# Squares of five norms and of the memory's queries and keys: summed by turning and adding along rows instead of by products with a column of ones

## The chip, the cores and the metric

The kernel runs on one core of a Trainium2 chip. The metric is the device time of one execution in microseconds. Before the change it is 3107.8 us, the median of three runs (3105.99 to 3108.2).

## What is computed

One layer of a first block and two layers of a second one, on 512 tokens of width 1024, all in float32. What matters here is the root-mean-square norm, which stands in front of or behind nearly every part:

```
def _rms(x, w):                      # x: tokens x features
    y = x * rsqrt(mean(x * x, axis=-1, keepdims=True) + EPS)
    return y * w

# memory attention, per head h of 4, width 256:
q = _rms((x @ w_in)[:, memory part].reshape(512, 4, 256), mem_q_norm)
k = _rms((_rms(mem) @ mem_w_kv)[:, :1024].reshape(256, 4, 256), mem_k_norm)

# second block, layer l:
h = h + rmsnorm(mix, gains[1])
h = h + rmsnorm(ff,  gains[3])
```

A norm thus needs, for each token, the sum of the squares over 1024 features (over 256 for each head of the memory's queries and keys).

## The kernel before

**Layout.** Activations are held with features on the 128 partitions and tokens along the row: a tile is 128 features x 512 tokens (256 for the memory). The sum over the features is therefore a sum over partitions and over tiles, and the factor of a token is wanted later in every partition.

**Products.** Each float32 product is made of three fp32r ones (high by high, high by low, low by high), recorded on line 752. Weights come in panels of 128x512 over one DMA queue; ScalarE makes the high half (WH, line 2176), GpSimd the low half (WL, line 2573).

**Order.** The program is a list of steps (PLAN, lines 363 to 531), in part written out by hand, which every engine walks through; LATE (532 to 566) moves single steps of VectorE, ScalarE or GpSimd to an earlier or later place in that engine's own order. Each engine's instructions are in order, and waits are semaphores with a mark per event. The eight PSUM banks are handed out by `lend` (line 718): the next tile gets the bank whose last reader comes earliest in the list, and TensorE waits for that reader.

**How a norm is summed.** ScalarE squares a tile. GpSimd adds tile on tile into one (`gather`, 2575). Then TensorE sums over partitions, step "fac":
- For norms whose last square arrives early enough, all tiles are gathered, TensorE turns the four 128x128 quarters (`across`, 816, recorded on line 819), and VectorE adds along the rows of the turned squares, 128x512 to 128x4 (`summed`, 1395, recorded on line 1398). Tokens then lie on partitions.
- For the five norms "nmem", "nab", "ns0", "nco", "ns1" the last square comes late and is not gathered. TensorE multiplies each quarter of the gathered squares by a column of ones (`columns`, 810, recorded on line 752 as PS<-VC,TMP 128x1), then waits for the last square and adds its quarters in the same PSUM columns. The result is one number per token, and VectorE reads it with one small operation (line 1385).
- For the memory's queries ("nqm", four heads) and keys ("nkm"), GpSimd adds the squares of the two tiles of a head in pairs; TensorE makes the columns of head p behind step "mq" or "mkl" 2p+2, the last head's in steps "nqm" and "nkm". One bank stays open for all heads. "nmem" and "nkm" have two quarters, as the memory has 256 tokens.

Behind the sum GpSimd raises it to the power -1/2 (`power`, 2583, line 2573, SM<-SM,VC). Step "bc" on TensorE broadcasts the factor by turning it (`spread`, 829, line 826, PS<-CST,SM), and VectorE's and ScalarE's work on the normed tiles goes on from there.

**The order at the sites of the change.** "ns0" and "ns1": a short product step "pf" 4, "fac", "pf" 5 (six products), "bc", "pf" 6 and 7, then the steps "grow". "nab" is alike, with "pf" 0 to 3. "nco": "fac" right behind the mixer's last product, then "pf" 1, "bc". "nmem": product "mkl" 0, "nqm", "fac", product "mkl" 1, "bc"; on VectorE LATE puts "fac" of "nmem" ahead of "nqm". On GpSimd "nqm" is first.

Of the kernel before, what the change touches and what calls it, by code (L numbers as in the profile page):

```python
# [16 lines left out]
EPS = 1e-6  # L17
# [565 lines left out]
def program(nc, x_in, mem_in, p_in, pos1, pos2, lam_in, vec_in, cst_in, dm_in, wst, out, total, dry=False):  # L583
    blocks = []
    with ExitStack() as ctx:
# [146 lines left out]
        def tensor(e):  # L732
# [77 lines left out]
            def columns(o, col, q, ind, first, nt=4):  # L810

                for t in range(nt):
                    z = mm(o[:, 64 * t + col:64 * t + col + ind.shape[1]], quarter(q, t), ind, first and t == 0, True)
                return z

            def across(o, q):

                for t in range(4):
                    z = e.transpose(quarter(o, t), quarter(q, t), ident)  # L819
                return z  # L820
# [23 lines left out]
            for marks.step, (kind, *i) in enumerate(PLAN):  # L844
                started.append(-(-len(blocks) // PT))
                if kind == "fac":
                    n = i[0]
                    K = NORM[n][2]
                    o = bank("var", n)
                    e.wait_ge(*at("gathered_fin" if n in ("nfin", "n1") else "gathered", n, last(n)))  # L850
                    if last(n) == K - 1:
                        across(o, sq(n, 0)).then_inc(*up("mm", "fac", n))
                    else:
                        columns(o, 0, sq(n, 0), one1, True, NORM[n][3])
                        e.wait_ge(*at("square", n, K - 1))
                        columns(o, 0, sq(n, K - 1), one1, False, NORM[n][3]).then_inc(*up("mm", "fac", n))
# [131 lines left out]
                elif kind == "mq":  # L988
                    m = i[0]
                    lin(("mq", m), ("mq", m), "w_in", 0, cc(O_MQ + 128 * m), range(8))  # L990
                    if m > 1 and m % 2 == 0:
                        if m == 2:
                            opened["nqm"] = bank("var", "nqm")
                        p = m // 2 - 1
                        e.wait_ge(*at("mq_pair", p))
                        columns(opened["nqm"], p, tmp(2 + 2 * (p % 2)), one1, p == 0).then_inc(*up("mm", "mq_sum", p))
                elif kind == "nqm":
                    e.wait_ge(*at("mq_pair", 3))
                    columns(opened["nqm"], 3, tmp(4), one1, False).then_inc(*up("mm", "mq_sum", 3))
# [8 lines left out]
                elif kind == "mkl":  # L1008
# [3 lines left out]
                    if m and m % 2 == 0:  # L1012
                        if m == 2:
                            opened["nkm"] = bank("var", "nkm")
                        p = m // 2 - 1
                        e.wait_ge(*at("mk_pair", p))
                        columns(opened["nkm"], p, tmp(2 + 2 * (p % 2)), one1, p == 0, 2).then_inc(*up("mm", "mk_sum", p))
                elif kind == "nkm":
                    e.wait_ge(*at("mk_pair", 3))
                    columns(opened["nkm"], 3, tmp(4), one1, False, 2).then_inc(*up("mm", "mk_sum", 3))  # L1020
# [356 lines left out]
        def vector(e):  # L1377
# [12 lines left out]
            def sums(n):  # L1390

                _, _, _, nt, nc_, _ = NORM[n]
                return psum("var", n)[:, 0:64 * nt].rearrange("p (t c) -> p t c", t=nt)[:, :, 0:nc_]

            def summed(n):

                e.wait_ge(*at("mm", "fac", n))
                e.reduce_sum(nsum(n)[:, :, 0], psum("var", n).rearrange("p (t c) -> p t c", c=128), AX).then_inc(*up("summed", n))
                e.wait_ge(*at("summed", n))
                return nsum(n)  # L1400

# [6 lines left out]
            def variance(n, done=None):  # L1408

                mult = NORM[n][1]  # L1410
                if n[0] in ("nr", "nk", "nd") and n[1] > 1:
                    e.wait_ge(*at("factor", (n[0], n[1] - 2)))
                if n[0] == "nd":
                    d_added(n[1], 0)
                    d_added(n[1], 1)
                    e.wait_ge(*at("d_added", n[1], 1))
                    stt(nwt(n, 0)[:, :, 2:4], nsum(n)[:, :, 2:4], mult, eps_mix[:, :, 2:4], MUL, ADD)
                    stt(nwt(n, 0)[:, :, 0:2], nsum(n)[:, :, 0:2], 64.0 * mult, eps_mix[:, :, 0:2], MUL, ADD).then_inc(*up("var", n))
                elif n[0] == "nq":
                    ts(nq_eps(n[1]), summed(n), 128.0 * EPS * mult, 128.0 * EPS * EPS, MUL, ADD).then_inc(*up("var", n))  # L1420
# [43 lines left out]
            for marks.step, _, (kind, *i) in turns("vector"):  # L1464
# [240 lines left out]
                elif kind == "mq":  # L1705
# [6 lines left out]
                    tt(ar(MQS[m]), psum("mq", m), RB, MUL).then_inc(*up("mq", m))  # L1712
                elif kind == "mg":
# [12 lines left out]
                elif kind == "nqm":  # L1726
                    variance("nqm", ("mq_sum", 3))
                    tt(mem_gain, VC[:, VOFF["mq"]:VOFF["mq"] + 2], VC[:, VOFF["mk"]:VOFF["mk"] + 2], MUL).then_inc(*up("mem_gain"))
                elif kind == "nkm":
                    variance("nkm", ("mk_sum", 3))  # L1730
# [1091 lines left out]
```

## Time and profile before

| | |
|---|---|
| median of three runs | 3107.8 us |
| profiled execution, its own time | 3109.54 us |
| its span | 3107.4 us |
| TensorE busy | 3067.1 us, 99% of the span |
| VectorE busy | 1108.6 us, 36% |
| ScalarE busy | 1251.3 us, 40% |
| GpSimd busy | 1717.8 us, 55% |
| mean granted TensorE clock | 0.998 |

Matmuls are pipelined and each record runs until its result is written, so the records overlap; the time that a group takes from TensorE is read from its first start to the start of what follows. Times in the rows are microseconds from the span's start. PE is TensorE, DVE VectorE, ACT ScalarE, POOL GpSimd.

### The profile page before, as it was taken

The page shows a single profiled execution, that of the slowest core. Times are in us where ns is not written, and L with a number is a line of the kernel's source. Part 1 is how long each engine was busy: PE and PEld are TensorE (multiplying, and loading weights), DVE is VectorE, ACT ScalarE, POOL GpSimd, SP SyncE. Part 2 cuts the span into 40 slices and gives each one's busy share as a digit, 9 for nine tenths or more (in the row PEclk, how much of TensorE's full clock was granted, in tenths as well). Part 3 has the DMA queues.
Part 4 walks back from the last instruction along what each step waited for, and adds up shares of the span by engine and source line. Part 5 has one row for each costly group of instructions (what it writes and reads, how often), then busy time and mean ns, then how long its engine had stood idle before and what let it go on. Part 6 is the DMA issues. An engine that isn't in the chain of part 4 may idle for free.

```text
span 3107.4 us, 40589 instructions
## 1 busy us (share of the span) xinstructions
PE 3067.1 (99%) x15246; PEld 2508.0 (81%) x15246; DVE 1108.6 (36%) x2097; ACT 1251.3 (40%) x2270; POOL 1717.8 (55%) x1359
## 2 busy tenths in 40 slices
PE   9999999999999999999999999999999999999999
PEld 7888877878777788788888878878888887788887
DVE  4322321223666522223222576533112259321124
ACT  4323332233555535343223433335333457643334
POOL 5555655565555466455555623347555664665554
PEclk9999999999999999999999999999999999999999
DMA  5333322322222234233333311123333331233332
GB/s 161 104 95 96 102 71 85 92 85 75 78 69 71 74 103 123 78 93 97 96 99 99 88 55 55 49 62 92 98 95 102 99 92 52 75 96 98 95 104 90
DMA packets 149840, 275.24 MB, mean 89 GB/s; under 512 B 16528, under 2 KB 17808, under 8 KB 149520
## 3 DMA queue, kind: packets, MB, share of 16 engines
q1 hardware_dynamic: 149648, 272.66, 30.6%
q8 instruction: 123, 2.02, 0.3%
q14 instruction: 69, 0.57, 0.1%
HBM read 270.50 MB, written 2.10 MB: 88 GB/s over the span
## 4 chain that ended last, share of the span: by engine, by line
PE 94%; DVE 4%; issue 1%; ACT 1%; POOL 1%; DMA 0%; SPq 0%; DVEq 0%; ACTq 0%; POOLq 0%
PE PS L752 91%; PE PS L826 2%; PE PS L819 1%; DVE AR L1382 1%; DVE TMP L1388 0%; DVE TMP L1382 0%; DVE PS L1382 0%; POOL WL L2573 0%; DVE AR L1388 0%; DMA RAW<-in_wst 0%; ACT AR L2176 0%; DVE ACC L1388 0%; DVE TMP L1385 0%; POOL SM L2573 0%; DVE Z L1388 0%
## 5 line engine op out<-in xcount | busy, mean ns | idle before, releaser
L2573 POOL TENSOR_TENSOR WL<-RAW,WH 128x512 fp32r<-128x512 f32 x1002 | 1295.9, 1305 | 791.8 <-ACT WH L2176 791.0
L2176 ACT ACTIVATE WH<-RAW 128x512 fp32r<-128x512 f32 x1002 | 619.8, 628 | 998.0 <-PE PS L752 937.3
L752 PE MATMUL PS<-HH,WH 128*128 128x512 f32 x2264 | 892.1, 394 | 3.9 <-ACT AR L2176 2.6
L752 PE MATMUL PS<-HH,WL 128*128 128x512 f32 x2264 | 882.5, 390 | 1.6 <-POOL WL L2573 1.5
L752 PE MATMUL PS<-HL,WH 128*128 128x512 f32 x2264 | 881.4, 389 | 0.0
L752 PE MATMUL PS<-AH,WH 128*128 128x512 f32 (+1 forms) x1504 | 582.3, 387 | 2.3 <-DVE AL L1382 1.2
L752 PE MATMUL PS<-AL,WH 128*128 128x512 f32 (+1 forms) x1504 | 579.6, 385 | 3.2 <-DVE AL L1382 2.3
L752 PE MATMUL PS<-AH,WL 128*128 128x512 f32 (+1 forms) x1504 | 579.3, 385 | 0.0
L752 PEld LDWEIGHTS PS<-HH,WH 128*128 128x128 f32 x2264 | 425.4, 188 | 93.7 <-issue 6.0
L752 PEld LDWEIGHTS PS<-HH,WL 128*128 128x128 f32 x2264 | 424.9, 188 | 92.2 <-POOL WL L2573 2.4
L752 PEld LDWEIGHTS PS<-HL,WH 128*128 128x128 f32 x2264 | 425.5, 188 | 85.5 <-DVE HL L1388 0.2
L752 PEld LDWEIGHTS PS<-AL,WH 128*128 128x128 f32 x1504 | 283.1, 188 | 61.3 <-DVE AL L1382 4.3
L752 PEld LDWEIGHTS PS<-AH,WH 128*128 128x128 f32 x1504 | 283.0, 188 | 60.5 <-issue 2.7
L752 PEld LDWEIGHTS PS<-AH,WL 128*128 128x128 f32 x1504 | 282.9, 188 | 56.4
L2573 POOL TENSOR_TENSOR AL<-TMP,AH 128x512 fp32r<-128x512 f32 x132 | 176.0, 1339 | 237.9 <-ACT AH L2176 237.9
L1382 DVE TENSOR_TENSOR TMP<-PS,RBT 128x512 f32<-128x512 f32 (+1 forms) x125 | 85.7, 690 | 475.7 <-PE PS L752 475.5
L752 PE MATMUL PS<-AR 64*64 64x64 f32 (+8 forms) x1652 | 217.2, 315 | 11.4 <-DVE AR L1463 3.6
L752 PEld LDWEIGHTS PS<-AR 64*64 64x64 f32 (+3 forms) x1652 | 149.5, 167 | 68.7 <-issue 39.6
L1382 DVE TENSOR_TENSOR ACC<-ACC,PS 128x512 f32<-128x512 f32 x136 | 93.5, 687 | 281.4 <-PE PS L752 281.4
L2573 POOL TENSOR_TENSOR TMP<-TMP 128x512 f32<-128x512 f32 (+1 forms) x92 | 117.9, 1281 | 87.2 <-ACT TMP L2176 85.6
L2573 POOL TENSOR_TENSOR SM<-SM,VC 128x4 f32<-128x4 f32 (+3 forms) x55 | 67.5, 1233 | 164.7 <-DVE SM L1388 122.1
L2176 ACT ACTIVATE TMP<-TMP 128x512 f32<-128x512 f32 x132 | 82.6, 626 | 179.6 <-DVE TMP L1388 134.4
(238 smaller groups left out, 2430.2 us busy)
## 6 DMA issues: line engine op xcount, KB each, us to landing
RAW<-in_wst SPq DMA_DIRECT2D x1002, 256.0 KB, 2.7
X<-in_x SPq DMA_DIRECT2D x8, 256.0 KB, 5.3
TMP<-in_p SPq DMA_DIRECT2D x8, 256.0 KB, 3.4
out<-X SPq DMA_DIRECT2D x8, 256.0 KB, 2.0
AR<-in_dm SPq DMA_DIRECT2D x1, 1024.0 KB, 6.4
AR<-in_mem SPq DMA_DIRECT2D x1, 1024.0 KB, 6.2
CST<-in_cst SPq DMA_DIRECT2D x1, 612.0 KB, 6.7
AR<-in_pos SPq DMA_DIRECT2D x2, 256.0 KB, 3.5
```

What stands on the lines that cost most here:

```text
L752: return e.matmul(o, l, r, start=a, stop=z, skip_group_check=True)
L819: z = e.transpose(quarter(o, t), quarter(q, t), ident)
L826: z = e.transpose(quarter(o, t), src(t), ident)
L1382: return e.tensor_tensor(o, a, b, op)
L2176: return e.activation(o, a, f, **kw)
L2573: return e.tensor_tensor(o, a, b, op)
```

## The change

All the products with a column of ones in these norms become turns, with the row sums made by VectorE:
- "fac" of the five norms: the gathered squares are turned into a bank of their own ("first_sum"); VectorE adds their rows and applies factor and epsilon. The last square is turned into the bank "var"; VectorE adds its rows and adds the first part in the operation that writes the variance.
- "nqm" and "nkm": each head's squares are turned into a bank of their own ("head_sum"), right where the columns were made; VectorE adds the rows in the steps "mq" and "mk" 2, 4 and 6 behind its product by the factor, and the last head's in "nqm" and "nkm".
- The order of the steps, the squares and the gathering on GpSimd, the powers and the broadcasts stay as they are.

```diff
-            def columns(o, col, q, ind, first, nt=4):
-                for t in range(nt):
-                    z = mm(o[:, 64 * t + col:64 * t + col + ind.shape[1]], quarter(q, t), ind, first and t == 0, True)
-                return z
-            def across(o, q):
-                for t in range(4):
+            def across(o, q, n=4):
+                for t in range(n):
                     z = e.transpose(quarter(o, t), quarter(q, t), ident)
                 return z
...
                 if kind == "fac":
-                    o = bank("var", n)
+                    whole = last(n) == K - 1
+                    o = bank("var" if whole else "first_sum", n)
                     e.wait_ge(*at("gathered_fin" if n in ("nfin", "n1") else "gathered", n, last(n)))
-                    if last(n) == K - 1:
-                        across(o, sq(n, 0)).then_inc(*up("mm", "fac", n))
-                    else:
-                        columns(o, 0, sq(n, 0), one1, True, NORM[n][3])
+                    across(o, sq(n, 0), NORM[n][3]).then_inc(*up("mm", "fac" if whole else "fac_first", n))
+                    if not whole:
+                        o = bank("var", n)
                         e.wait_ge(*at("square", n, K - 1))
-                        columns(o, 0, sq(n, K - 1), one1, False, NORM[n][3]).then_inc(*up("mm", "fac", n))
+                        across(o, sq(n, K - 1), NORM[n][3]).then_inc(*up("mm", "fac", n))
...
                     if m > 1 and m % 2 == 0:
-                        if m == 2:
-                            opened["nqm"] = bank("var", "nqm")
                         p = m // 2 - 1
+                        o = bank("head_sum", "nqm", p)
                         e.wait_ge(*at("mq_pair", p))
-                        columns(opened["nqm"], p, tmp(2 + 2 * (p % 2)), one1, p == 0).then_inc(*up("mm", "mq_sum", p))
+                        across(o, tmp(2 + 2 * (p % 2))).then_inc(*up("mm", "mq_sum", p))
...
+            def head_sum(n, h):
+                e.wait_ge(*at("mm", {"nqm": "mq_sum", "nkm": "mk_sum"}[n], h))
+                o = psum("head_sum", n, h)[:, 0:128 * NORM[n][3]].rearrange("p (t c) -> p t c", c=128)
+                e.reduce_sum(nsum(n)[:, :, h], o, AX).then_inc(*up("head_sum", n, h))
...
-                elif n == "nqm":
-                    e.wait_ge(*at("mm", *done))
-                    ts(nwt(n, 0), sums(n), 256.0 * mult, 256.0 * EPS, MUL, ADD).then_inc(*up("var", n))
+                elif n in ("nqm", "nkm"):
+                    head_sum(n, 3)
+                    e.wait_ge(*at("head_sum", n, 3))
+                    a = 256.0 if n == "nqm" else 1.0
+                    ts(nwt(n, 0), nsum(n), a * mult, a * EPS, MUL, ADD).then_inc(*up("var", n))
                 else:
-                    e.wait_ge(*at("mm", *(done or ("fac", n))))
-                    ts(nwt(n, 0), sums(n), mult, EPS, MUL, ADD).then_inc(*up("var", n))
+                    e.wait_ge(*at("mm", "fac_first", n))
+                    o = psum("first_sum", n)[:, 0:128 * NORM[n][3]].rearrange("p (t c) -> p t c", c=128)
+                    e.reduce_sum(nwt(n, 1)[:, :, 0], o, AX).then_inc(*up("first_sum", n))
+                    e.wait_ge(*at("first_sum", n))
+                    ts(nwt(n, 2), nwt(n, 1), mult, EPS, MUL, ADD).then_inc(*up("first_var", n))
+                    summed(n)
+                    e.wait_ge(*at("first_var", n))
+                    stt(nwt(n, 0), nsum(n), mult, nwt(n, 2), MUL, ADD).then_inc(*up("var", n))
...
                     tt(ar(MQS[m]), psum("mq", m), RB, MUL).then_inc(*up("mq", m))
+                    if m > 1 and m % 2 == 0:
+                        head_sum("nqm", m // 2 - 1)
...
                     tt(mkv[:, m, :], psum("mk", m)[:, 0:256], RBM, MUL).then_inc(*up("mk", m))
+                    if m > 1 and m % 2 == 0:
+                        head_sum("nkm", m // 2 - 1)
```

The edits of "mkl", "nqm" and "nkm" on TensorE are like those of "mq".

## Rows read from the trace of the kernel before

**Rows 1.** The page: the span, and its chain that ended last, by engine.
```profile
span 3107.4 us, 40589 instructions
...
PE 94%; DVE 4%; issue 1%; ACT 1%; POOL 1%; DMA 0%; SPq 0%; DVEq 0%; ACTq 0%; POOLq 0%
```

**Rows 2.** Groups by form: records, busy us, mean ns, idle before (TensorE, then VectorE).
```profile
L752 PE MATMUL PS<-VC,TMP 128*128 128x1 f32 x120 | 14.4, 243 | 0.7 <-ACT TMP L2176 0.7
...
L1747 DVE TENSOR_REDUCE SM<-PS 128x1 f32<-128x256 f32 x16 | 6.7, 417 | 0.5 <-PE PS L752 0.4
```

**Rows 3.** Timeline at step "mq" 2: start, us, instruction, records, idle before.
```profile
1087.70 0.94 PE L752 MATMUL PS<-VC,TMP 128*128 128x1 f32 x8
1088.51 0.74 PE L826 MATMUL PS<-CST,AR 128*128 128x128 f32 x5
...
1094.98 0.69 DVE L1382 TENSOR_TENSOR AR<-PS,RBT 128x512 f32<-128x512 f32 x1 [6.38 <-PE PS L752]
```

**Rows 4.** Timeline at "fac" and "bc" of "ns0".
```profile
2472.91 1.84 PE L752 MATMUL PS<-VC,TMP 128*128 128x1 f32 x16
...
2474.61 0.49 PE L752 MATMUL PS<-HH,WH 128*128 128x512 f32 x1
...
2474.79 0.16 DVE L1385 TENSOR_SCALAR SM<-PS 128x4 f32<-128x4 f32 x1 [2.35 <-PE PS L752]
...
2475.03 1.02 POOL L2573 TENSOR_TENSOR SM<-SM,VC 128x4 f32<-128x4 f32 x1
...
2476.10 0.65 PE L826 MATMUL PS<-CST,SM 128*128 128x128 f32 x4
```

**Rows 5.** Timeline at "fac" of "nf1", a norm that is turned already.
```profile
2723.07 0.60 PE L819 MATMUL PS<-CST,TMP 128*128 128x128 f32 x4
...
2723.43 0.47 PE L752 MATMUL PS<-HH,WH 128*128 128x512 f32 x1
...
2723.71 0.69 DVE L1398 TENSOR_REDUCE SM<-PS 128x4 f32<-128x512 f32 x1 [6.26 <-PE PS L819]
...
2724.43 0.17 DVE L1385 TENSOR_SCALAR SM<-SM 128x4 f32<-128x4 f32 x1
```

**Rows 6.** Timeline, TensorE: "bc" of "nmem", and the columns of "nkm" head 1.
```profile
1173.96 0.43 PE L826 MATMUL PS<-CST,SM 128*128 128x128 f32 x2 [1.05 <-POOL SM L2573]
1174.14 0.36 PE L752 MATMUL PS<-AH,WH 128*128 128x256 f32 x1
...
1184.90 0.50 PE L752 MATMUL PS<-VC,TMP 128*128 128x1 f32 x4
1185.27 0.36 PE L752 MATMUL PS<-AH,WH 128*128 128x256 f32 x1
```

**Rows 7.** Timeline, TensorE: the second set of "nco" and its "bc".
```profile
2693.99 1.05 PE L752 MATMUL PS<-VC,TMP 128*128 128x1 f32 x8 [0.65 <-ACT TMP L2176]
...
2696.40 0.65 PE L826 MATMUL PS<-CST,SM 128*128 128x128 f32 x4
```

**Rows 8.** Timeline at "nqm" and "nmem"; the last row from the chain, GpSimd's powers.
```profile
1167.98 1.95 PE L752 MATMUL PS<-VC,TMP 128*128 128x1 f32 x16
...
1169.96 0.24 DVE L1385 TENSOR_SCALAR SM<-PS 128x2 f32<-128x2 f32 x2 [4.07 <-PE PS L752]
...
1170.38 3.54 POOL SM L2573 x2
```

**Rows 9.** Two waits, then stretches (busy us and records by engine, PEclk), a third wait.
```profile
1336.92 0.47 PE L752 MATMUL PS<-AH,WH 128*128 128x512 f32 x1 [0.87 <-ACT AH L2176]
1338.16 0.50 PE L752 MATMUL PS<-AL,WH 128*128 128x512 f32 x1 [0.77 <-DVE AL L1382]
...
1339.20:1342.60 3.40, 3.40 (x10) 2.63 (x9) 3.12 (x6) 1.74 (x4) 1.58 (x1) 0.50 0.00 0
1342.60:1346.00 3.40, 3.40 (x16) 2.80 (x15) 0.66 (x1) 0.63 (x1) 2.16 (x2) 0.99 0.30 86
...
1808.61 0.50 PE L752 MATMUL PS<-HH,WL 128*128 128x512 f32 x1 [1.50 <-POOL WL L2573]
```

More of the change, by code:

```diff
@@ L991, in tensor @@
                     if m > 1 and m % 2 == 0:
-                        if m == 2:
-                            opened["nqm"] = bank("var", "nqm")
                         p = m // 2 - 1
+                        o = bank("head_sum", "nqm", p)
                         e.wait_ge(*at("mq_pair", p))
-                        columns(opened["nqm"], p, tmp(2 + 2 * (p % 2)), one1, p == 0).then_inc(*up("mm", "mq_sum", p))
+                        across(o, tmp(2 + 2 * (p % 2))).then_inc(*up("mm", "mq_sum", p))
                 elif kind == "nqm":
+                    o = bank("head_sum", "nqm", 3)
                     e.wait_ge(*at("mq_pair", 3))
-                    columns(opened["nqm"], 3, tmp(4), one1, False).then_inc(*up("mm", "mq_sum", 3))
+                    across(o, tmp(4)).then_inc(*up("mm", "mq_sum", 3))
                 elif kind == "mg":
@@ L1012, in tensor @@
                     if m and m % 2 == 0:
-                        if m == 2:
-                            opened["nkm"] = bank("var", "nkm")
                         p = m // 2 - 1
+                        o = bank("head_sum", "nkm", p)
                         e.wait_ge(*at("mk_pair", p))
-                        columns(opened["nkm"], p, tmp(2 + 2 * (p % 2)), one1, p == 0, 2).then_inc(*up("mm", "mk_sum", p))
+                        across(o, tmp(2 + 2 * (p % 2)), 2).then_inc(*up("mm", "mk_sum", p))
                 elif kind == "nkm":
+                    o = bank("head_sum", "nkm", 3)
                     e.wait_ge(*at("mk_pair", 3))
-                    columns(opened["nkm"], 3, tmp(4), one1, False, 2).then_inc(*up("mm", "mk_sum", 3))
+                    across(o, tmp(4), 2).then_inc(*up("mm", "mk_sum", 3))
                 elif kind == "mkn":
@@ L1388, in stt @@
                 return e.scalar_tensor_tensor(out=o, in0=a, scalar=s, in1=b, op0=op0, op1=op1)
-            def sums(n):
-                _, _, _, nt, nc_, _ = NORM[n]
-                return psum("var", n)[:, 0:64 * nt].rearrange("p (t c) -> p t c", t=nt)[:, :, 0:nc_]
             def summed(n):
                 e.wait_ge(*at("mm", "fac", n))
-                e.reduce_sum(nsum(n)[:, :, 0], psum("var", n).rearrange("p (t c) -> p t c", c=128), AX).then_inc(*up("summed", n))
+                e.reduce_sum(nsum(n)[:, :, 0], psum("var", n)[:, 0:128 * NORM[n][3]].rearrange("p (t c) -> p t c", c=128), AX).then_inc(*up("summed", n))
                 e.wait_ge(*at("summed", n))
                 return nsum(n)
+            def head_sum(n, h):
+                e.wait_ge(*at("mm", {"nqm": "mq_sum", "nkm": "mk_sum"}[n], h))
+                o = psum("head_sum", n, h)[:, 0:128 * NORM[n][3]].rearrange("p (t c) -> p t c", c=128)
+                e.reduce_sum(nsum(n)[:, :, h], o, AX).then_inc(*up("head_sum", n, h))
             def d_added(h, j):
@@ L1406, in d_added, with variance @@
                 e.reduce_sum(nsum(("nd", h))[:, :, 2 * j:2 * j + 2], o, AX).then_inc(*up("d_added", h, j))
-            def variance(n, done=None):
+            def variance(n):
                 mult = NORM[n][1]
@@ L1726, in vector @@
                 elif kind == "nqm":
-                    variance("nqm", ("mq_sum", 3))
+                    variance("nqm")
                     tt(mem_gain, VC[:, VOFF["mq"]:VOFF["mq"] + 2], VC[:, VOFF["mk"]:VOFF["mk"] + 2], MUL).then_inc(*up("mem_gain"))
                 elif kind == "nkm":
-                    variance("nkm", ("mk_sum", 3))
+                    variance("nkm")
                 elif kind == "mk":
```

## The prediction, made before the change was run

> **What bounds the kernel now.** I read the page's chain first: TensorE carries 94% of the chain that ended last [rows 1], so an instruction taken from TensorE is worth its time wherever TensorE does not wait. Next the groups by form: the 128x1 products with the column of ones are 120 records [rows 2]; an fp32 product leaves two, so these are 60 products. They make up twelve sets of four quarters (two sets in each of "nab", "ns0", "nco", "ns1", four in "nqm") and six sets of two quarters (two in "nmem", four in "nkm"). That is all that the change removes; it puts as many turns and some reductions on VectorE in their place. Last I read the timeline at each site, to see what stands behind the sets. There are two kinds: sets whose sum is wanted much later, and sets that the next broadcast ("bc") waits for.
>
> **The price of a set.** Four quarters of products took from 1087.70 to 1088.51, 0.81 us, before TensorE began the next thing [rows 3]; in pairs 1.70 us, 0.85 each [rows 4]. Four turns with the identity, as the kernel does them elsewhere, took from 2723.07 to 2723.43, 0.36 us [rows 5]. A set of four gets 0.45 us shorter. Two quarters: 0.37 us as products (1184.90 to 1185.27) and 0.18 as turns (1173.96 to 1174.14) [rows 6], so 0.19 less. All of it together would be 12 x 0.45 + 6 x 0.19 = 6.5 us. The question is how much of it is kept.
>
> **The price of adding on VectorE.** In rows 5 the reduction of 128x512 starts 0.64 us behind the first turn, takes 0.69, and the small operation behind it starts 0.03 later and takes 0.17. Today's small operation reads the finished sum at once: 2474.79, 0.16 us [rows 4].
>
> **Part 1, queries, sets 0 to 2 (steps "mq" 2, 4, 6).** TensorE is on the path and nothing near needs the sum: 3 x 0.45 = **1.35 us saved**. VectorE gets a reduction of 0.69 each and waits for the turns first; these end while it still multiplies "mq" 2 by the factor, so that wait is short. What is queued behind it: after that product VectorE stood idle for 6.38 us, and its next work began at 1094.98 [rows 3], so 0.7 to 1.4 us fit. If that cover were gone, the scores' maxima behind it would come up to 0.8 us later, three times.
>
> **Part 2, keys (steps "mk", "nkm").** Four sets of two: 4 x 0.19 = **0.76 us saved**. Their reductions run in an idle VectorE. After the last one TensorE has four steps of "mv" before "mkn"; a step is six products of 512, which take 1.49 us in rows 4, so there are 6 us for a chain that grows by 0.7. Without that cover it would cost 0.7 us.
>
> **Part 3, norms "nab", "ns0", "ns1".** Rows 4 show the present chain from the first product: both sets to 2474.61, VectorE at 2474.79 for 0.16, GpSimd's power at 2475.03 for 1.02, the broadcast at 2476.10. That is 3.19 us. Six products of the "pf" step run in it and end just as the factor comes, so the broadcast follows on with no idle time: the two paths are level. With the change, counted from the first turn: first reduction 0.64 to 1.33, its scaling 1.36 to 1.53, second reduction 1.56 to 2.25 (its turns were ready at 1.00, VectorE was not), last operation 2.28 to 2.45, power 2.53 to 3.55, broadcast 3.60. TensorE is through with its six products at 2.2 and then waits 1.4 us. The 0.9 us saved is gone and the broadcast is 0.4 us later. TensorE and VectorE both go on from the broadcast, so it stays lost: **3 x 0.4 = 1.2 us lost**.
>
> **Part 4, norm "nco".** Its second set waits for the last square until 2693.99, broadcast at 2696.40 [rows 7]. The first reduction fits into that wait. From 2693.99: reduction at +0.63, end +1.32, last operation to +1.52, power +1.60 to +2.62, broadcast +2.67 against 2.41 now: **0.27 us lost**, and all of the saving with it.
>
> **Part 5, "nmem" and the last set of the queries.** TensorE does "nqm" set 3 and both sets of "nmem" in one run from 1167.98; VectorE reads at 1169.96; GpSimd is busy until 1170.38 with weights and then computes both powers in 3.54 us, and the broadcast waited 1.05 us for them [rows 8, 6]. Here GpSimd sets the time. After: VectorE's order is "nmem" first. Its first turns are readable at about 1168.8 (0.36 later than the run's start, and 0.46 for two turns); a reduction of 128x256 is taken as 0.42 us, from a like reduction of 256 elements [rows 2]. Then: 1168.80, reduction to 1169.22, scaling to 1169.42, reduction to 1169.87, last operation to 1170.07, the 128x512 reduction of "nqm" to 1170.79, its scaling to 1170.99, GpSimd at 1171.07 instead of 1170.38. **0.7 us lost.** Behind the two powers GpSimd has the low halves of the next weights; they move back by 0.7 us too, and TensorE, which stands at the broadcast meanwhile, does not want them sooner. TensorE arrives 0.8 us earlier and the factor comes 0.7 later: it waits 1.05 + 0.8 + 0.7 = 2.6 us.
>
> **Part 6, the clock.** TensorE's granted clock fell to 0.50, the lower level of 1.2 GHz, from 1339.2 to 1342.6 after waits of 0.87 and 0.77 us [rows 9]. In that stretch 10 products ran, in the next of the same length 16. The six missing are worth 6 x 0.21 = 1.3 us; half of 3.4 us at half the clock is 1.7. I take 1.6 for such a stretch. A wait of 1.50 us at 1808.61 was followed by none [rows 9]. For the cost of the 2.6 us wait there are thus two ends, 0 and 1.6; I take **1.6 us**, since 2.6 is well over the 1.64 after which it fell. For the 1.4 us waits of part 3 I take 0, by the row at 1808.61.
>
> **Banks.** The extra banks are taken from the ones released longest ago. Following the rule of `lend`, each new tenant's predecessor in these steps has been read several us before. I take 0; the upper end would be one reduction, 0.7 us, at a few sites.
>
> **Sum:** -1.35 - 0.76 + 1.2 + 0.27 + 0.7 = +0.05, and with the clock +1.7 us. The profiled execution took 3109.54 us (span 3107.4), which is 1.7 over the median of 3107.8; on the median the forecast is 3107.8 + 1.7 = **3109.5 us**. A measurement of this kernel can tell about 0.2% (6.2 us) from no change, so this is no change.
>
> **Rivals.**
> Level: as above, but the clock stays at 2.4 GHz behind the wait in "nmem": 3107.8 + 0.05, 3107.9 us. For it: the clock also stood at its upper level behind the wait of 1.50 us, so a wait alone does not settle it. Chance 0.28.
> All is kept: the added reductions hide, broadcasts come earlier than now. 3107.8 - 6.5 = 3101.3 us, faster by 0.21%. For it: TensorE at 94% of the chain. Against it: the broadcast in rows 4 comes 0.05 us behind GpSimd's power, so it is the factor's chain that decides. Chance 0.06.
> Slower, by the clock: the wait at each of the five broadcasts takes the clock to 1.2 GHz, each time for 1.6 us: 3107.8 + 0.05 + 8 = 3115.9 us. It decides from four of the five on (6.4 us). For it: 1.4 us of waiting is near the 1.64 that preceded a fall, and "nco" waits twice, for its last square and for the factor. Against it: 1808.61. Chance 0.06. The Trainium skill (TensorE: Matmul & The Clock Gate, Part 4, PE-mode transpose) says that turns do not count as TensorE activity for its clock gate as products do. That speaks against this change and for this rival, since every removed product becomes a turn; no row before shows a turn's effect by itself.
> Between: one or two falls more than the one in the sum, 3111 to 3113 us. Chance 0.10. The forecast itself has 0.50.
>
> **Numbers.** Range 3103.5 to 3113.0: below it takes in the level case (3107.9) and most of the way on to "all is kept"; above, two more falls (3109.5 + 3.2) and a little. Faster 0.06, same 0.87, slower 0.07.
>
> **What would show it.** Right: records of 128x1 only for "m_d"; sets of turns 0.36 to 0.41 us long; a TensorE wait of 1.0 to 1.5 us for GpSimd at the four broadcasts, where there is none now, and of 2.6 us at that of "nmem"; a stretch of clock 0.50 behind the latter; VectorE reductions two by two with no gap. Wrong: broadcasts of "ns0" and "ns1" under 3.2 us after their first turn, or a wait for VectorE at the scores behind "mq" 2.

## The result, and the profile after

The changed kernel took 3114.89 us (median of 19 runs, 3108.93 to 3116.69), the kernel before beside it 3108.86 us (3105.99 to 3113.49). The ratio is 1.0016, with a 95% interval of 1.0010 to 1.0023: slower by 5 us, where +1.7 us was forecast, and above the range (3103.5 to 3113.0). By the bound of 0.2% it is no change, as forecast; the size is wrong. Measured twice more later, each time beside its own runs of before, the ratio was 1.0005 (0.9996 to 1.0014) and 1.0012 (1.0003 to 1.0021). The mean of the three is 1.0011, or +3.4 us. The medians alone scatter more: +6.0, -0.4 and +4.3 us against their own runs of before, and the interval of the second measurement does not exclude 1. What has to be explained is thus a cost of 3 to 4 us, which the profiles show at the sites of the change each time, and a part of the first measurement that is not there each time.

The page of the changed kernel, its first line and TensorE's busy time; TensorE had 3067.1 us before. TensorE does less and the span is 6.2 us longer [rows 1]:

```profile
span 3113.6 us, 40508 instructions
...
PE 3063.7 (98%) x15186; PEld 2503.3 (80%) x15186; DVE 1121.2 (36%) x2120; ACT 1251.1 (40%) x2270; POOL 1717.8 (55%) x1359
```

The waits of TensorE (who waited, for whom, us in total, times, longest). The top line is new; the kernel before waited for GpSimd's factor once, for the 1.05 us in [rows 6]:

```profile
PE PS L820 <- POOL SM L2580: 8.9, 5, 3.5
```

Five waits for the factor, 8.9 us in all: 3.46 at "nmem", 1.54 at "nab", 1.62 at "ns0" and "ns1", 0.69 at "nco". The timeline at "ns0", which answers to [rows 4]. Line 813 is `across`, 1426 and 1387 are the two reductions, 1379 the scaling between them, 1382 the last operation, 2580 GpSimd, 820 the broadcast:

```profile
2477.13 1.04 PE L813 MATMUL PS<-CST,TMP 128*128 128x128 f32 x8
2477.76 0.69 DVE L1426 TENSOR_REDUCE SM<-PS 128x4 f32<-128x512 f32 x1 [1.12 <-PE PS L813]
2477.91 1.29 POOL L2580 TENSOR_TENSOR WL<-RAW,WH 128x512 fp32r<-128x512 f32 x1 [0.69 <-ACT WH L2183]
2477.92 0.47 PE L752 MATMUL PS<-HH,WH 128*128 128x512 f32 x1
...
2478.49 0.74 DVE L1379 TENSOR_SCALAR SM<-SM 128x4 f32<-128x4 f32 x1
...
2479.14 0.68 DVE L1387 TENSOR_REDUCE SM<-PS 128x4 f32<-128x512 f32 x1
...
2479.86 0.16 DVE L1382 SCALAR_TENSOR_TENSOR SM<-SM 128x4 f32<-128x4 f32 x1
2480.10 1.02 POOL L2580 TENSOR_TENSOR SM<-SM,VC 128x4 f32<-128x4 f32 x1 [0.89 <-DVE SM L1382]
2481.17 0.65 PE L820 MATMUL PS<-CST,SM 128*128 128x128 f32 x4 [1.62 <-POOL SM L2580]
```

The scaling of four numbers takes 0.74 us, not 0.17; all other operations last within 0.01 us of the forecast. GpSimd's instruction began at 2477.91 and ended at 2479.20; the scaling began at 2478.49 and ended at 2479.23, 0.03 us behind it. The broadcast comes 4.04 us after the first turn; forecast 3.60, before 3.19.

The timeline at "nmem" and "nqm", which answers to [rows 8] and [rows 6]:

```profile
1166.56 2.52 POOL L2580 TENSOR_TENSOR WL<-RAW,WH 128x512 fp32r<-128x512 f32 x2
1166.75 1.06 PE L813 MATMUL PS<-CST,TMP 128*128 128x128 f32 x8
1167.63 0.42 DVE L1426 TENSOR_REDUCE SM<-PS 128x2 f32<-128x256 f32 x1 [3.07 <-PE PS L813]
...
1168.09 1.02 DVE L1379 TENSOR_SCALAR SM<-SM 128x2 f32<-128x2 f32 x1
1169.02 0.41 DVE L1387 TENSOR_REDUCE SM<-PS 128x2 f32<-128x256 f32 x1
1169.47 0.16 DVE L1382 SCALAR_TENSOR_TENSOR SM<-SM 128x2 f32<-128x2 f32 x1
1169.55 0.69 DVE L1395 TENSOR_REDUCE SM<-PS 128x4 f32<-128x512 f32 x1
...
1170.52 3.57 POOL L2580 TENSOR_TENSOR SM<-SM,VC 128x16 f32<-128x16 f32 x2 [1.44 <-DVE SM L1379]
1174.06 2.53 POOL L2580 TENSOR_TENSOR WL<-RAW,WH 128x512 fp32r<-128x512 f32 x2
1174.15 0.43 PE L820 MATMUL PS<-CST,SM 128*128 128x128 f32 x2 [3.46 <-POOL SM L2580]
```

The same thing: the scaling of two numbers takes 1.02 us and ends at 1169.11, GpSimd's two instructions at 1169.08. Everything behind it on VectorE, and the powers, are late by that. Then the clock, a stretch behind the broadcast (columns as in [rows 9]):

```profile
1175.20:1178.60 3.40, 3.40 (x18) 3.40 (x17) 0.63 (x2) 1.90 (x4) 3.40 (x5) 0.50 0.56 149
```

The clock granted there is 0.50, in the kernel before it was 1.00, with 29 products in the stretch instead of 18.

### The profile page after: what moved, and what is told of

The parts are those of the page before. It is cut to its first block, busy times and chain, and to the rows that moved or that the text cites. A ratio compares the mean times of both kernels' runs of the same rounds, so it can differ in the third digit from the quotient of the medians.

```text
span 3113.6 us, 40508 instructions
## 1 busy us (share of the span) xinstructions
PE 3063.7 (98%) x15186; PEld 2503.3 (80%) x15186; DVE 1121.2 (36%) x2120; ACT 1251.1 (40%) x2270; POOL 1717.8 (55%) x1359
## 4 chain that ended last, share of the span: by engine, by line
PE 95%; DVE 3%; issue 1%; POOL 1%; ACT 0%; DMA 0%; DVEq 0%; ACTq 0%; POOLq 0%
PE PS L752 92%; PE PS L820 2%; PE PS L813 1%; DVE AR L1376 1%; DVE TMP L1382 0%; POOL SM L2580 0%; DVE PS L1376 0%; ACT AR L2183 0%; DVE TMP L1376 0%; DVE SM L1387 0%; DVE ACC L1382 0%; DVE AR L1382 0%; DVE Z L1382 0%; DVE SM L1379 0%; DVE TMP L1379 0%
```

## The experiments

Each lists its edit against the changed kernel unless it says otherwise; the cuts leave out lines that only move semaphores. To compare places, the instructions with which ScalarE makes the high halves are matched one by one (1002 in every trace): how far each comes behind its like in the trace of before. Differences of these over a stretch are the cost of the stretch. At 1087 us, ahead of any edit, the traces already stand -0.4 to +1.3 us from that of before, so single spans say little.

**Heads alone, norms alone.** e1 keeps the columns in the five norms; e2 keeps them in queries and keys.

```diff
 # e1, step "fac":
-across(o, sq(n, 0), NORM[n][3]) ... across(o, sq(n, K - 1), NORM[n][3])
+columns(o, 0, sq(n, 0), one1, True, NORM[n][3]) ... columns(o, 0, sq(n, K - 1), one1, False, NORM[n][3])
 # e2, steps "mq", "nqm", "mkl", "nkm":
-across(o, tmp(2 + 2 * (p % 2)))
+columns(opened["nqm"], p, tmp(2 + 2 * (p % 2)), one1, p == 0)
```

> Only the sets of the queries and keys are turned; the five norms keep their products with ones. Theory (the loss sits in the norms' longer chains and in the clock behind the wait of nmem): the savings of parts 1 and 2 stay, about 2 us faster than before, the broadcasts of nab, ns0 and ns1 3.2 us after their first product as before, and no stretch of clock 0.50 near 1175. Rival (any shift of TensorE's work moves the stretches of low clock further back, and these make the difference): about as slow as the changed kernel, 4 to 5 us over before, though the broadcasts are in time.

> Only the five norms are turned; the queries and keys keep their products with ones. Theory: all the loss and none of the savings, 5 to 7 us slower than before: the broadcasts of nab, ns0, ns1 about 4.0 us after their first turn, nmem's factor late and clock 0.50 behind its wait. Rival (the queries' reductions on VectorE delay the memory part): near before, under 3 us slower.

Measured: e1 3107.7 us, ratio 0.9993 (0.9984 to 1.0002); e2 3114.62 us, ratio 1.0013 (1.0004 to 1.0022). The cost needs the norms, but the two parts do not simply add up. By place (as in the table further down, without the stretch that has no edit) e1 gains 2.2 us, e2 loses 3.5, and the changed kernel loses 3.2 and not 1.3. The difference is at "nmem": e2 waits 2.34 us there and no low clock stands behind it, which its expectation had wrong. With the last set of the queries turned as well, TensorE is earlier and the powers are later, the wait is 3.46 us, and the clock falls. The 4.8 us of e2 by the medians are near the 5 to 7 expected, but 1.5 of them lie where no kernel has an edit.

**"nmem" alone with columns** (e4).

> The changed kernel, but nmem alone keeps its products with ones. Theory: GpSimd starts the two powers 1.1 us sooner, TensorE waits about 2 us at nmem's broadcast instead of 3.46, and the clock stays at 1.00 behind it; 2.5 us faster than the changed kernel. If the clock falls behind 2 us as well, only 1.1 us faster. Rival (nmem's delay is hidden later): as slow as the changed kernel.

Measured: 3108.9 us, ratio 0.9998 (0.9989 to 1.0007). The wait at "nmem" is 1.74 us instead of 3.46 and no low clock stands behind it. The four other norms are as in the changed kernel, with waits of 1.52 to 1.62 us at the broadcasts of three. By place e4 is 2.5 us under the changed kernel (+0.7 against +3.2), as expected for the case that the clock stays up.

**Why the scaling is slow**, three ways. e3 keeps the first sum in PSUM, so that the scaling has its source there. e10 puts it behind the second reduction. e11 leaves VectorE alone and moves GpSimd's power ahead of the low half of the weights in "nab", "ns0" and "ns1".

```diff
 # e3
-e.reduce_sum(nwt(n, 1)[:, :, 0], o, AX)
+k = psum("first_sum", n)[:, 0:NORM[n][3]].rearrange("p (t c) -> p t c", c=1)
+e.reduce_sum(k[:, :, 0], o, AX)
-ts(nwt(n, 2), nwt(n, 1), mult, EPS, MUL, ADD)
+ts(nwt(n, 2), k, mult, EPS, MUL, ADD)
 # e10
-ts(nwt(n, 2), nwt(n, 1), mult, EPS, MUL, ADD).then_inc(*up("first_var", n))
 summed(n)
+ts(nwt(n, 2), nwt(n, 1), mult, EPS, MUL, ADD).then_inc(*up("first_var", n))
 # e11, LATE of GpSimd
+("fac", "nab"): -1, ("fac", "ns0"): -1, ("fac", "ns1"): -1,
```

> The changed kernel, but the first sum is written into PSUM and its scaling reads it there, not from SBUF. Theory (a scaling from SBUF to SBUF on VectorE stands still until GpSimd's running instruction has ended; one that reads PSUM does not): the scaling takes 0.16 to 0.17 us at all five norms instead of 0.65 to 1.02; the broadcasts of nab, ns0, ns1 come 3.5 us after the first turn instead of 4.0; about 2 us faster than the changed kernel. Rival (the scaling is slow because it follows a reduction or because of its size): it stays at 0.65 to 1.0 us and nothing is gained.

> The changed kernel with the scaling of the first sum moved behind the reduction of the last square, nothing else. Theory of contention (the 128x4 scaling from SBUF to SBUF waits until GpSimd's running instruction has ended): at ns0 and ns1 the second reduction now starts at once behind the first and ends 1.4 us after it began, when GpSimd's low-half instruction (it ends 2.07 us behind the first turn) is over too; the scaling takes 0.17 to 0.25 us there, the broadcast comes 3.6 us behind the first turn against 4.04, and the three norms give back 1.3 us: 3113.6 us. Rival (the scaling is slow whatever GpSimd does, by its source or its place): it takes 0.74 us again, the broadcast stays at 4.04 or later, and the time stays at 3114.9.

> The changed kernel with GpSimd's order alone changed: at nab, ns0 and ns1 the power comes before the low half of the weights that ran beside the scaling (that panel is wanted much later). VectorE's instructions and their order are untouched. Theory of contention: with GpSimd idle the scaling takes 0.17 us at these three sites; counted from the first turn the broadcast comes at 3.5 to 3.6 us against 4.04, and the time falls by about 1.4 us, to 3113.5. Rival: the scaling stays at 0.74 us with GpSimd idle, and the broadcast at 4.04.

The timeline at "ns0" in e3 (its lines 1427 and 2581 answer to 1426 and 2580):

```profile
2472.86 1.04 PE L813 MATMUL PS<-CST,TMP 128*128 128x128 f32 x8
2473.50 0.70 DVE L1427 TENSOR_REDUCE PS<-PS 128x4 f32<-128x512 f32 x1 [1.12 <-PE PS L813]
2473.64 1.29 POOL L2581 TENSOR_TENSOR WL<-RAW,WH 128x512 fp32r<-128x512 f32 x1 [0.70 <-ACT WH L2184]
...
2474.23 0.16 DVE L1379 TENSOR_SCALAR SM<-PS 128x4 f32<-128x4 f32 x1
...
2476.34 0.65 PE L820 MATMUL PS<-CST,SM 128*128 128x128 f32 x4 [1.05 <-POOL SM L2581]
```

The same in e10:

```profile
2476.33 1.04 PE L813 MATMUL PS<-CST,TMP 128*128 128x128 f32 x8
...
2477.11 1.29 POOL L2580 TENSOR_TENSOR WL<-RAW,WH 128x512 fp32r<-128x512 f32 x1 [0.69 <-ACT WH L2183]
2477.69 0.69 DVE L1387 TENSOR_REDUCE SM<-PS 128x4 f32<-128x512 f32 x1
2478.42 0.17 DVE L1379 TENSOR_SCALAR SM<-SM 128x4 f32<-128x4 f32 x1
...
2479.94 0.65 PE L820 MATMUL PS<-CST,SM 128*128 128x128 f32 x4 [1.19 <-POOL SM L2580]
```

And in e11, where GpSimd does nothing at the time (its lines 814, 1427, 1380 and 821 answer to 813, 1426, 1379 and 820):

```profile
2469.97 1.04 PE L814 MATMUL PS<-CST,TMP 128*128 128x128 f32 x8
2470.61 0.69 DVE L1427 TENSOR_REDUCE SM<-PS 128x4 f32<-128x512 f32 x1 [1.12 <-PE PS L814]
2471.34 0.17 DVE L1380 TENSOR_SCALAR SM<-SM 128x4 f32<-128x4 f32 x1
...
2473.45 0.65 PE L821 MATMUL PS<-CST,SM 128*128 128x128 f32 x4 [1.05 <-POOL SM L2581]
```

In e3 the scaling runs in the middle of GpSimd's instruction, as in the changed kernel, and takes 0.16: with its source in PSUM it does not wait. In e10 and e11 source and operation are those of the changed kernel and GpSimd's instruction is over or not there: 0.17. The broadcast comes 3.48, 3.61 and 3.48 us after the first turn. The times are 3111.65, 3110.34 and 3111.64 us, ratios 1.0004 (0.9995 to 1.0013), 1.0003 (0.9994 to 1.0012) and 1.0008 (0.9999 to 1.0016): in the expected direction, but the runs alone would not have told 1 us from nothing. The traces tell it: from 2111 us on the changed kernel loses 2.7 us, e3 and e11 1.1. e10 loses 1.7, since its scaling stands in the path at "nco" too. And by place e3 is level with before: -0.2 us in all (table below). At "nmem" it loses 0.7 us and not 2.55, as the wait there is 2.93 us and the clock does not fall. One thing stays slow in e3 at "nmem": the last operation, whose two inputs both lie in SBUF, starts during GpSimd's instruction and takes 0.47 us instead of 0.16.

**The low clock at "nmem"** (e9, and once more as e14): TensorE waits busy.

```diff
 elif kind == "bc" and i[0] == "nmem":
     o = bank("rb", "nmem")
+    for _ in range(12):
+        mm(o, HH[:, 0, 0:128], HH[:, 1, :], True, True)
     e.wait_ge(*at("factor", "nmem"))
```

> The changed kernel with 12 products more (128x512, into the bank that the broadcast of nmem will overwrite) in front of TensorE's wait for the factor of nmem, so that it waits busy (12 x 0.23 = 2.8 of 3.5 us). Theory that the wait's low clock costs time: the stretch of clock 0.50 behind that broadcast (1175.2 in the changed kernel) is gone, and from the broadcast to 1216 TensorE needs 1.1 to 1.6 us less, so the median is 3113.3 to 3113.8 us against 3114.9. Rival, the fall of the clock comes and goes from execution to execution and costs the median little: the time stays within 1 us of the changed kernel's. If the twelve products delay the broadcast itself (they should end before the factor), the time grows by what they overrun.

Measured: 3110.98 us, ratio 1.0002 (0.9993 to 1.0011). The broadcast comes at 1174.15, as in the changed kernel, and the stretch behind it is at full clock:

```profile
1175.20:1178.60 3.40, 3.40 (x29) 3.23 (x29) 1.48 (x4) 2.44 (x6) 3.40 (x5) 1.00 0.42 116
```

Between 1167 and 1186 this kernel loses 1.25 us and the changed kernel 2.55: the low clock costs 1.3. The median was 3.9 us under the changed kernel's, though, more than that. So both ran again, beside one another:

> The changed kernel once more, beside the three that follow, for its time on this chip and a second profile. If the low clock behind the broadcast of nmem belongs to the wait of 3.46 us there, it stands at about 1175 again; the low stretches between 1330 and 2050 stand behind waits that the change does not touch, and may be other ones than in the first profile. Time within 1 us of 3114.9 and of the ratio 1.0016.

> The changed kernel with twelve products in front of the wait at nmem, once more, beside the changed kernel on the same chip. In the first profile of it the stretch behind nmem was gone and 1.3 us less passed there, while the median was 3.9 us lower than the changed kernel's on another chip. If the low clock at nmem is all that the twelve products take away, the difference to the changed kernel is 1.3 to 1.6 us here; if other low stretches go with it, it is 3 us or more.

Measured: the changed kernel 3110.96 us, with the fill 3112.81 us, both 1.0005 of before. The changed kernel came 3.9 us under its first median, outside what was expected for it, and the fill was 1.9 us above it instead of 1.3 to 1.6 below: the medians do not resolve this edit. By place the two runs of the fill do agree: at "nmem" the fill loses 1.24 us, 1.25 the first time. What the profiles show is steady: the wait at "nmem" is 3.46 to 3.47 us in all three profiles of the changed kernel, with clock 0.50 behind it, and 2.55 us are lost there in two, 3.7 in the third (e20), where the low clock lasted twice as long.

What is not steady lies between 1334 and 2111 us, where no kernel here has an edit. Low stretches of 3.4 us stand there behind one wait or another, two to five in a profile of the changed kernel and four in that of before. The stretch of time came out +3.10, -3.33 and +0.18 us against before in the three profiles of the changed kernel, +0.09 and +3.05 with the fill, +1.48 and +1.46 in e1 and e2, +1.43 in e18 below, which has no turned set at all: steps of about 1.6 us. All profiles fit one count: 1.6 us for each low stretch, except that one at about 1769 us costs next to nothing. TensorE waits for VectorE at about 1789 us anyway, 2.15 to 2.19 us without that stretch and 0.86 with it (the lines are of before and of the changed kernel):

```profile
1789.25 0.59 PE L752 MATMUL PS<-SC,CST 128*128 128x16 f32 x4 [0.86 <-DVE SC L1385]
...
1789.51 0.52 PE L752 MATMUL PS<-SC,CST 128*128 128x16 f32 x2 [2.17 <-DVE SC L1379]
```

Counting a double stretch as two, before has such a stretch and three that cost time; the first profile of the changed kernel has five that do, e13 one, e20 three and e18 four. Half of the first profile's 6.2 us is this.

**GpSimd's order at "nmem".** Its queries' power takes 2.91 us and is wanted 40 us later. e16 only swaps it with that of "nmem"; e17 moves it behind the norm of the keys, and e18 does the same in the kernel before.

```diff
 # LATE of GpSimd
+("fac", "nmem"): -2,      # e16
+("nqm",): 29,             # e17, and e18 in the kernel before
```

> The changed kernel with GpSimd's order alone changed: it computes nmem's power (0.70 us) ahead of that of the queries' heads (2.91 us), whose factor is wanted 40 us later. Theory that GpSimd's two powers set the broadcast of nmem: nmem's variance is there at 1169.6, its factor at 1170.4, TensorE reaches the broadcast at 1170.7 and does not wait (3.46 us in the changed kernel), no clock 0.50 stands behind it, and the time falls by 3.5 + 1.3 = 4.8 us, to about 3110. Rival: TensorE runs into the low halves of the weights, which GpSimd still computes behind the powers, and waits there instead; then 1 to 3 us less are gained.

> The changed kernel with the queries' power (2.91 us on GpSimd) moved behind the keys' norm, where its factor is still wanted later. Theory that GpSimd's work sets the time from nmem to the keys' pairs: neither the broadcast of nmem (3.46 us in the changed kernel) nor the keys' first pair (4.46 us with nmem's power first) makes TensorE wait more than 0.5 us, no clock 0.50 stands at 1175, and at 1218 TensorE is 4 us or more ahead of the changed kernel. Rival: another wait takes its place (the low halves of the weights, or the scores for the queries' factor), and less than 2 us are gained there.

> The kernel before with the queries' power moved behind the keys' norm in the same way. The broadcast of nmem waits 1.05 us for GpSimd there; that goes: at 1218 it is 1.0 us ahead of before, time 0.9995 to 0.9998 of before. Against the changed kernel with the same move it shows what the change costs without the site of nmem: by the traces -1.35 - 0.76 - 0.4 + 2.9 (norms) = +0.4 us. Rival: nothing gained, since GpSimd is late for the keys' pairs instead.

e16 took 3113.31 us, ratio 1.0008 (0.9999 to 1.0017). Its timeline, GpSimd and the turn of the keys' first pair:

```profile
1172.31 2.90 POOL L2581 TENSOR_TENSOR SM<-SM,VC 128x16 f32<-128x16 f32 x1
...
1175.17 2.49 POOL L2581 TENSOR_TENSOR WL<-RAW,WH 128x512 fp32r<-128x512 f32 x2
...
1177.62 0.73 POOL L2581 TENSOR_TENSOR TMP<-TMP 128x256 f32<-128x256 f32 x1
...
1178.49 0.66 PE L814 MATMUL PS<-CST,TMP 128*128 128x128 f32 x2 [4.46 <-POOL TMP L2581]
```

The expectation failed: the broadcast no longer waits, but the keys' first pair does, 4.46 us, since the same 2.90 us now stand in front of GpSimd's sum of that pair. The wait only moved, and the low clock went with it (from 1177.4). GpSimd's work bounds this part. e17 takes it away:

```profile
1170.21 0.38 PE L820 MATMUL PS<-CST,SM 128*128 128x128 f32 x2
...
1172.58 0.74 POOL L2580 TENSOR_TENSOR TMP<-TMP 128x256 f32<-128x256 f32 x1
...
1173.47 0.41 PE L813 MATMUL PS<-CST,TMP 128*128 128x128 f32 x2
```

No wait, no low clock there, and by 1334 us 4.6 us less than in the changed kernel (table below): 3109.06 us, ratio 0.9996 (0.9988 to 1.0005). e18 took 3109.97 us, 0.9997 (0.9989 to 1.0006), and its trace is 1.5 us ahead over the site. With the wait at "nmem" taken out of both, changed and unchanged kernel are level: by place e17 is 0.2 us behind e18, where 0.4 was expected.

**A third measurement of the change** (e20):

> The changed kernel a third time. The forecast's terms with the scaling and the nmem wait as measured give +2.0 us of norms, queries and keys and +1.3 of clock, +3.3 us or 1.0011; the first two measurements were 1.0016 and 1.0005. If the low stretches at unchanged waits differ by execution and not by kernel, this one lies between 1.0003 and 1.0018 again.

3114.22 us, ratio 1.0012 (1.0003 to 1.0021), within what was expected.

**Versions that should beat both.** e12: queries and keys turned; "nmem" and "nco" by columns; in "nab", "ns0" and "ns1" the gathered squares turned and the last square by columns, the first sum in PSUM, GpSimd's power ahead of the low half. e15 adds "nmem" turned with its first sum in PSUM, and its power first; e19 has the queries' power behind the keys' norm instead.

```diff
 # e12, step "fac"
 across(o, sq(n, 0), NORM[n][3]).then_inc(*up("mm", "fac_first", n))
-across(o, sq(n, K - 1), NORM[n][3]).then_inc(*up("mm", "fac", n))
+columns(o, 0, sq(n, K - 1), one1, True, NORM[n][3]).then_inc(*up("mm", "fac", n))
 # VectorE: both read from PSUM (k as in e3)
+ts(nwt(n, 2), k, mult, EPS, MUL, ADD)
+stt(nwt(n, 0), o, mult, nwt(n, 2), MUL, ADD)
```

> A version that should beat both kernels. Heads of queries and keys turned as in the change; nmem and nco as before the change; in nab, ns0 and ns1 the gathered squares are turned and added on VectorE while TensorE sums the last square by the column of ones, whose result VectorE reads at once; the first sum stays in PSUM; GpSimd computes the power before the low half of the weights. Expected from the first turn: turns 0.36, columns to 1.21, read 0.18 later at 1.39; first reduction 0.64 to 1.33, scaling to 1.53, last operation to 1.73, power 1.80 to 2.82, broadcast 2.88 against 3.19 before. That is 0.3 us at each of three norms on top of the heads' gain: 0.9 us under the version with the heads alone (3107.7, with before at 3109.8), so 3106.8 us, 0.1% under before. Rival, GpSimd's low half still stands in front of the power: the broadcast stays at 3.15 to 3.19 and the time is that of the heads alone.

> The version that should beat both: the mixed one (heads turned; in nab, ns0 and ns1 the gathered squares turned and the last square by the column of ones; first sum in PSUM; nco by columns) and, beyond it, nmem turned with its first sum in PSUM and its power ahead of the queries' on GpSimd. The mixed version took 3107.8 with before at 3109.85. TensorE's wait at nmem (1.74 us in the mixed version) goes, and 0.38 us of products: 3105.7 us, 0.13% under before. Rival: the wait comes back as one for the low halves of the weights, and the time is that of the mixed version.

> The version that should beat both: heads turned, nmem turned with its first sum in PSUM, nab, ns0 and ns1 mixed (gathered squares turned, last square by the column of ones, GpSimd's power ahead of the low half), nco by columns, and the queries' power behind the keys' norm. By the terms measured: heads -2.1, nmem's products -0.4 and its wait -1.05, the three norms -0.25 each: 4.3 us under before, ratio 0.9986. Rival: GpSimd's work at nmem keeps 2 us of it (as when only nmem's power came first), ratio 0.9993.

e12 took 3107.84 us, ratio 0.9991 (0.9982 to 1.0000). e15 took 3108.86, 0.9999 (0.9990 to 1.0008): the wait of 4.46 us for the keys' first pair is in it as in e16, and takes what was gained elsewhere. e19 took **3103.23 us, ratio 0.9978 (0.9969 to 0.9988)**, faster than both. Expected were 4.3 us under before; the median is 6.7 under; by place it is 3.5 under, or 5.0 without one low stretch at "nco". In the stretch without an edit it happens to be 1.6 us ahead too. Its timeline at "ns0":

```profile
2466.90 0.60 PE L820 MATMUL PS<-CST,TMP 128*128 128x128 f32 x4
2467.33 0.95 PE L753 MATMUL PS<-VC,TMP 128*128 128x1 f32 x8
2467.54 0.70 DVE L1447 TENSOR_REDUCE PS<-PS 128x4 f32<-128x512 f32 x1 [1.11 <-PE PS L820]
2468.27 0.16 DVE L1395 TENSOR_SCALAR SM<-PS 128x4 f32<-128x4 f32 x1
2468.54 0.17 DVE L1398 SCALAR_TENSOR_TENSOR SM<-PS,SM 128x4 f32<-128x4 f32 x1
2468.78 1.02 POOL L2607 TENSOR_TENSOR SM<-SM,VC 128x4 f32<-128x4 f32 x1 [1.78 <-DVE SM L1398]
...
2469.85 0.65 PE L827 MATMUL PS<-CST,SM 128*128 128x128 f32 x4
```

The reduction runs beside the columns, and the broadcast comes at 2.95 us, without a wait. (In e12 it came at 3.31 at "ns0": VectorE's last operation stood 0.35 us later there than at the two other norms. The cause is open; it is not so in e15 and e19.)

## Why the prediction was off

The cost by place, in us against before, from the matched instructions. In the forecast's column "nmem" is 0.7 + 1.6, the norms 1.2 + 0.27:

```
                          forecast  after  e13    e20    e9 fill  e3 psum  e17    e19
sets of queries, to 1167   -1.35    -1.27  -1.27  -1.26  -1.27    -1.26    -1.27  -1.27
"nmem", 1167 to 1186       +2.3     +2.55  +2.55  +3.73  +1.25    +0.71    -2.42  -2.62
keys, 1186 to 1334         -0.76    -0.74  -0.67  -0.73  -0.75    -0.72    -0.36  -0.32
no edit, 1334 to 2111       0       +3.10  -3.33  +0.18  +0.09    +1.50    +1.39  -1.60
four norms, from 2111      +1.47    +2.66  +2.69  +2.57  +2.72    +1.08    +2.80  +0.71
```

(e13 and e20 are the changed kernel again. The 0.71 of e19 holds 1.5 us of a low stretch at "nco", behind the wait for its last square.)

**Parts 1 and 2 held** to 0.1 us: a set of four turned is 0.40 to 0.46 us shorter, the keys' four sets 0.7 together, and the reductions cost nothing. VectorE is idle for 5.4 us behind the one of "mq" 2.

**The step that failed is in parts 3 and 5: "its scaling 1.36 to 1.53", and the scaling of 0.20 us in "nmem".** It was priced by [rows 5], where no GpSimd instruction runs. Measured it is 0.65, 0.74 and 0.74 us at "nab", "ns0" and "ns1", and 1.02 at "nmem". Behind it second reduction, last operation, power and broadcast are late: the broadcast stands 3.95 us behind the first turn at "nab" and 4.04 at "ns0" and "ns1", 0.35 and 0.44 over the forecast. The cleanest measure is e11, which has the same instructions on VectorE in the same order: its broadcast at "ns0" comes at 3.48 us, so the contention costs 0.56. The forecast was thus 0.12 too long elsewhere: it let the second reduction start behind the end of the scaling, but in e11 it starts 0.07 us after the scaling's start (2471.34, 2471.41). That e10 comes at 3.61, right at the forecast's 3.60, is another order with a sum of the same size. Part 4 had "nco" at +0.27 and it cost 0.3 to 0.4 in the three profiles; GpSimd is idle there, the scaling took 0.17, and the broadcast came 2.71 us after the second set began (2.67 forecast).

The trace of before had shown the effect, in rows that I did not read. Its group of small scalings (busy us, mean ns) is slower than the 0.17 us of most of them (the slowest, at 1753.51, takes 1.22):

```profile
L1385 DVE TENSOR_SCALAR SM<-SM 128x4 f32<-128x4 f32 x20 | 5.0, 249 | 0.7
```

and one of the slow ones stands in "nf0", another turned norm, next to what delays it:

```profile
2539.26 1.30 POOL L2573 TENSOR_TENSOR WL<-RAW,WH 128x512 fp32r<-128x512 f32 x1 [1.42 <-ACT WH L2176]
2539.39 0.69 DVE L1398 TENSOR_REDUCE SM<-PS 128x4 f32<-128x512 f32 x1 [8.09 <-PE PS L819]
2540.11 0.47 DVE L1385 TENSOR_SCALAR SM<-SM 128x4 f32<-128x4 f32 x1
```

GpSimd ends at 2540.56, the scaling at 2540.58. The Trainium skill (SBUF — State Buffer, Who interferes with whom) names the mechanism: VectorE and GpSimd share a pair of ports as an exclusive lock, and `tensor_scalar` in its two-port modes takes it, while a reduction does not, nor a VectorE instruction with at most one SBUF input outside those modes. The traces agree in this: the reduction kept its 0.69 us beside the same instruction of GpSimd, and the scaling from PSUM its 0.16. That the lock is what holds the scaling up is the reading of the Trainium skill; the runs show only that it waits for GpSimd's instruction, and that it does not with its source in PSUM. The Trainium skill here speaks against this change, and the forecast should have had its rule as a rival.

**Part 6 came true, but in part by luck.** A stretch at 1.2 GHz stands behind the wait at "nmem" in all three profiles, 1.3 us by the fill against 1.6 taken. But the wait was 3.46 us and not 2.6; the scaling is 0.8 of that difference. Behind the waits of 2.34 us (e2) and 2.93 us (e3) at the same place no low clock stood, so the wait of 2.6 us that was forecast might well have had none: by these single profiles, it was the slow scaling that made the wait long enough. Taking 0 behind the norms' waits held too: 0.69 to 1.62 us at four broadcasts in three profiles, and no low stretch from 2110 to 3100 in any of them. So the rival in which all five fall is refuted. For the Trainium skill's rule on turns and the clock this is no test, as the turns are few and stand next to waits.

**The sum.** -1.27 + 2.55 - 0.74 + 2.66 = +3.2 us, or 1.0010, against 1.0016, 1.0005 and 1.0012 measured. Of the 1.5 us over the forecast 1.2 are in the four norms and 0.25 at "nmem", where two misses cancel: 1.25 us against 0.7 without the clock, 1.3 against 1.6 for it. With the scaling out of GpSimd's way (e3) the sum by place is -0.2 us: the slow scaling, with the fall of the clock at "nmem" that came with it, is the whole cost in that profile, and without it the rival "level" (+0.05; its terms add up to +0.06) would have come true. The rest of the first measurement's 5 us are low stretches at waits that the change leaves alone; whether the change makes them more frequent is not settled, as three profiles with two to five of them can't tell. The rival "one or two more falls" was near in time (3111 to 3113); the first profile did have two more that cost time, but behind waits without an edit, and over the three profiles they cancel (+3.1, -3.3, +0.2). The base counts too: 3107.8 us was the median of three runs, and the kernel before took 3108.9 to 3111.3 in all later ones. The range was too narrow: I took in falls of the clock but gave the price of a small VectorE operation no upper bound, though it had been read at one place only.

## What to carry to other kernels

A duration read at one place holds only beside the same neighbours. When small VectorE operations are added to a path, look at what GpSimd runs at that moment, and keep their source in PSUM or put them where GpSimd is idle; in the groups, a mean above the usual duration is the hint. A wait for an in-order engine that is busy throughout moves when two of its instructions are swapped, and goes only when work leaves the stretch. And where a kernel's low-clock stretches come and go by themselves, cost an edit by place, from matched instructions, before reading the medians.

## What the runs showed of the hardware

- A scaling of 128x4 or 128x2 from SBUF to SBUF that starts while GpSimd's 1.3 us instruction on SBUF runs takes the rest of that instruction and 0.03 us (0.47, 0.65, 0.74, 1.02 and 1.22 measured), and 0.17 where less than 0.15 us is left; with its source in PSUM it takes 0.16 in the same place. The one of 128x8 in the keys' norm took 0.91 in the changed kernel (at 1209.74), off TensorE's path. Scalings of 128x1 did not wait: 27 in the kernel before began during an instruction of GpSimd and took 0.21 us, like the 53 others. An operation on two inputs in SBUF waited in e3 (128x2, 0.47 us), but one of 128x4 that began with 0.47 us of a power on GpSimd left took 0.16 (1757.70 in the kernel before): not explained.
- The low clock stood behind the waits of 3.13 us and more at "nmem" or the keys' first pair, and behind none of 2.93 and less there (1.05, 1.74, 2.34, 2.93), with one profile each for 1.05, 2.34, 2.93 and 3.13; elsewhere it followed waits of 0.8 us [rows 9], in some executions and not in others. Twelve products in the wait kept the clock up.
